# Rotary parts on 128 rows with pages turned in pairs, and GLA level scores written by predicated copies, in a two-layer MLA and GLA step

## The chip, the core and the metric

The kernel runs on one core of a Trainium2 chip. The metric is the device time of one execution in microseconds (us). A core has TensorE (PE, with its weight loads shown apart as PEld), VectorE (DVE), ScalarE (ACT), GpSimd (POOL) and SyncE (SP), each with its own instruction queue, and semaphores between them.

## What is computed

One inference step of two layers. Each layer is FFN half-step, token mixer, FFN half-step, with an RMSNorm before and after each part. Layer 0 mixes by multi-head latent attention (MLA), layer 1 by gated linear attention (GLA). There are 512 prompt tokens and 8 x 8 new tokens of sequences with 2048 cached positions in 16 pages each; model width 1024.

```python
# MLA, prompt: 8 heads, 128 plain and 64 rotary columns
s = (jnp.einsum('bqhd,bkhd->bhqk', qn, k_nope)
     + jnp.einsum('bqhr,bkr->bhqk', qp, k_pe)).astype(jnp.float32) * MLA_SCALE
# MLA, new tokens: latent cache (256) and rotary cache (64), pages by page_table
past_ckv = cache_ckv[page_table].reshape(B, -1, MLA_KV_LORA).astype(c_kv.dtype)
past_kpe = cache_kpe[page_table].reshape(B, -1, MLA_ROPE).astype(k_pe.dtype)
s = (jnp.einsum('bthr,bkr->bhtk', q_lat, all_ckv)
     + jnp.einsum('bthd,bkd->bhtk', q_pe, all_kpe)).astype(jnp.float32) * MLA_SCALE
# GLA: 4 heads, keys of 128, values of 256
diff = G[:, :, None] - G[:, None, :]
decay = jnp.exp(jnp.where(causal[None, :, :, None, None], diff, -jnp.inf))
attn = jnp.sum(qf[:, :, None] * kf[:, None, :] * decay, axis=-1)
```

## The kernel before

**Layout and stages.** Activations are held transposed, features on the 128 partitions and the 576 tokens along the free axis in two halves of 288. Six stages follow each other: FFN, MLA, FFN, FFN, GLA, FFN. Nearly all work is a stream of weight blocks of 128x1024: SP loads a block into `raw` (four slots), ACT writes its high part `w_hi` (L526), POOL its low part `w_lo` (L875), and TensorE forms each product by three matmuls (L1550 to L1552). An output of 288 columns is a *unit*; units go round six PSUM banks, counted by `s_unit` (made by TensorE) and `s_evicted` (emptied by DVE). Every engine's program is written out by hand in stage order; an engine waits on a semaphore, and what is queued behind waits with it.

**MLA, projection.** After the query, key and value blocks, DVE builds the rotary query part `qpe` (64 rows, L1204 to L1208, one sum per head and half, `s_rope`), then copies the new tokens' columns of each head to `q_pes` (L1213, eight copies, `s_qpes`), then empties the key (`kn`, L1218) and value (`vp`, L1223) units. POOL's queue holds only `low(n)` for each block, in order: six down blocks, eight query blocks (uq), two of uk, two of uv.

**MLA, prompt attention.** For 32 steps (8 heads, 4 query blocks of 128, 128 to 512 keys) TensorE forms scores by a product over 128 rows (L1789) and one over the 64 rotary rows (L1790) into one bank, two steps ahead of the transposes of the probabilities (L1815); every fourth step `head_out` follows (L1797). DVE masks (L1245), takes the maximum (L1248), and scales the exponentials (L1258); ACT does the exponential (L708) and copies the transposes (L720).

**MLA, decode.** Batches go in four pairs, each with four groups of four pages. `load_pages` (L361) puts pages into `cache` (four buffers), per group two pages by SP's queue and two by POOL's. For a batch and a group (32 *part-groups*) TensorE transposes the pages: four of 128x128 for each latent half (L1844) and four of 128x64 for the rotary part (L1847), into banks 4, 5 and 6. DVE copies bank 4 (L1268), ACT banks 5 and 6 (L734), to `c_t`. The next part-group's transposes wait for those copies (`s_ctv`, `s_cta`). `group_scores` then forms, for both batches of the pair side by side on 64 columns each, two latent products (L1860) and one over 64 rotary rows (L1862). After four groups come the softmax, the transposes of the probabilities and the products with the pages (L1916). `new_scores` (L1876, L1878) does the same for the eight new tokens.

**GLA.** The chunk scores are made level by level: for each head seven levels (`halves`, L347, splits the tokens into blocks of 2b and compares the second half with the first), and an eighth unit, the diagonal one, which needs no `xl`. A level's operand `xl` (three buffers) takes a difference per half on DVE (`level_dif`, L1358 and L1359), one exponential on ACT (L778), and the products with q on DVE (`q_mul`, L1366) and with k on POOL (`k_mul`, L912). It is begun two levels ahead: at level unit x, DVE issues the difference of x+2, empties unit x, and issues the q product of x+2. TensorE's unit (L1998) waits for both products (L1990 to L1992). DVE empties a unit by a product with the level's 0/1 mask: level 0 into `att_p`, the others into one of two `masked` buffers (L1439), which POOL adds to `att_p` (L933, `g_att`). Levels 4 and up also have a 64-column unit for the new tokens (L2000, L1452; POOL's sum L939, `g_att_s`). The order of the stage is a plan made at build time (L311 to L334): 13 projection blocks (j = 12 to 24) and between them 32 level units, in bursts of two or three:

```python
while j >= 12 and spread and (j + 1 - 12) * (GH * (LEVELS + 1)) > (GH * (LEVELS + 1) - len(spread)) * (GLA_IN - 12):
    kind, hd, lv = spread.pop(0)
    g_plan.append((kind, hd, lv))
```

This gives bursts of 3, 2, 3, 2, 3, 2, 3, 2, 3, 2, 3, 2, 2. POOL takes the `low` of a block (L875) where the plan has that block, between the burst before it and the burst behind it.

## Time and profile before

| | us |
|---|---|
| median of 3 runs (2517.78 to 2524.62) | 2523.54 |
| the profiled execution's own time | 2515.44 |
| its span, first to last instruction | 2513.8 |
| PE busy | 2439.3 (97%) |
| DVE busy | 1019.4 (41%) |
| POOL busy | 852.2 (34%) |
| ACT busy | 789.8 (31%) |

TensorE is busy nearly throughout; matmuls are pipelined, so a busy TensorE isn't one at its peak, and the distance from one start to the next tells more than a duration. The mean granted clock is 0.990 of full speed. FP32 matmuls appear as two records each, transposes as one. Of the chain that ended last 88% is TensorE and 8% DVE.

### The profile page before, as it was taken

What the parts mean: (1) busy time and instruction counts of PE and PEld (TensorE: products, weight loads), DVE (VectorE), ACT (ScalarE), POOL (GpSimd) and SP (SyncE); (2) the same over time, 40 slices, a digit from 0 to 9 for tenths busy, and PEclk for the clock granted to TensorE, in tenths of its full rate; (3) what the DMA queues carried; (4) which work ended last, traced back from release to release, by engine and by line L of the source; (5) the groups of instructions that cost most, each with busy time, mean ns of one, the idle gap of its engine ahead of it and who ended that gap; (6) DMA issues with size and microseconds to landing.
All of it is one profiled execution on the core that took longest, in us unless ns stands there. A gap on an engine that the chain in (4) does not pass through costs nothing.

```text
span 2513.8 us, 43938 instructions
## 1 busy us (share of the span) xinstructions
PE 2439.3 (97%) x17572; PEld 2299.7 (91%) x17572; DVE 1019.4 (41%) x1919; ACT 789.8 (31%) x1392; POOL 852.2 (34%) x477
## 2 busy tenths in 40 slices
PE   8999999899899999999999999999999999999997
PEld 8999999895456999999999999999988799999997
DVE  5332222686332643332254332126577666323223
ACT  5222222414332442222243222224321444222221
POOL 3333333120221133333314333331467423333332
PEclk9999999999999999999999999999999999999999
DMA  3222222130551232222213222222211322222222
GB/s 123 84 84 83 80 84 80 58 115 1 164 172 34 60 91 80 81 83 85 82 58 96 84 80 81 83 86 78 68 51 51 143 85 68 84 83 83 79 86 76
DMA packets 68648, 209.04 MB, mean 83 GB/s; under 512 B 8380, under 2 KB 21181, under 8 KB 68254
## 3 DMA queue, kind: packets, MB, share of 16 engines
q1 hardware_dynamic: 65438, 196.58, 25.5%
q0 software_dynamic: 3072, 10.49, 1.5%
q8 instruction: 103, 1.69, 0.3%
q14 instruction: 35, 0.29, 0.0%
HBM read 199.22 MB, written 7.82 MB: 82 GB/s over the span
## 4 chain that ended last, share of the span: by engine, by line
PE 88%; DVE 8%; ACT 1%; issue 1%; POOL 1%; DMA 0%; POOLq 0%; SPq 0%; DVEq 0%
PE psum L1550 25%; PE psum L1552 25%; PE psum L1551 25%; PE psum L1844 1%; PE psum L1860 1%; DVE h L1016 1%; PE psum L1916 1%; DVE y_ffn L1012 1%; PE psum L1998 1%; DVE x_lo L986 1%; PE psum L1790 1%; DVE work L1007 1%; PE psum L1789 1%; PE psum L1797 1%; DVE w_lo L995 1%
## 5 line engine op out<-in xcount | busy, mean ns | idle before, releaser
L875 POOL TENSOR_TENSOR w_lo<-raw,w_hi 128x1024 fp32r<-128x1024 f32 (+2 forms) x315 | 734.7, 2334 | 1420.0 <-ACT w_hi L526 1420.0
L1550 PE MATMUL psum<-x_hi,w_hi 128*128 128x288 f32 x3568 | 1072.9, 301 | 21.9 <-DVE x_lo L986 17.7
L1552 PE MATMUL psum<-x_hi,w_lo 128*128 128x288 f32 x3568 | 1053.9, 295 | 0.0
L1551 PE MATMUL psum<-x_lo,w_hi 128*128 128x288 f32 x3568 | 1052.9, 295 | 0.0
L1550 PEld LDWEIGHTS psum<-x_hi,w_hi 128*128 128x128 f32 x3568 | 671.7, 188 | 38.5 <-DVE x_lo L986 27.4
L1551 PEld LDWEIGHTS psum<-x_lo,w_hi 128*128 128x128 f32 x3568 | 671.9, 188 | 3.7
L1552 PEld LDWEIGHTS psum<-x_hi,w_lo 128*128 128x128 f32 x3568 | 671.4, 188 | 0.0
L526 ACT ACTIVATE w_hi<-raw 128x1024 fp32r<-128x1024 f32 (+2 forms) x331 | 341.4, 1033 | 797.9 <-DMA raw<-ffn_in 364.2
L1032 DVE TENSOR_TENSOR work<-psum,r_pre 128x288 f32<-128x288 f32 x352 | 160.3, 457 | 659.5 <-PE psum L1552 659.0
L1550 PE MATMUL psum<-gu_hi,w_hi 128*128 128x288 f32 x1408 | 415.5, 295 | 0.0
L1552 PE MATMUL psum<-gu_hi,w_lo 128*128 128x288 f32 x1408 | 414.7, 295 | 0.0
L1551 PE MATMUL psum<-gu_lo,w_hi 128*128 128x288 f32 x1408 | 414.6, 294 | 0.0
L1550 PEld LDWEIGHTS psum<-gu_hi,w_hi 128*128 128x128 f32 x1408 | 264.2, 188 | 0.2
L1551 PEld LDWEIGHTS psum<-gu_lo,w_hi 128*128 128x128 f32 x1408 | 264.1, 188 | 0.2
L1552 PEld LDWEIGHTS psum<-gu_hi,w_lo 128*128 128x128 f32 x1408 | 264.1, 188 | 0.0
L1037 DVE COPY y_ffn<-psum 128x288 f32 (+1 forms) x60 | 27.1, 452 | 366.9 <-PE psum L1552 366.9
L565 ACT ACTIVATE gu_hi<-work 128x288 f32 (+1 forms) x176 | 76.9, 437 | 224.6 <-DVE work L1053 224.6
L1053 DVE TENSOR_TENSOR work<-work 128x288 f32<-128x288 f32 x176 | 116.0, 659 | 28.6 <-ACT work L561 11.5
L561 ACT ACTIVATE work<-work 128x288 f32<-128x288 f32 x176 | 76.3, 436 | 134.0 <-DVE work L1032 133.9
L1048 DVE TENSOR_TENSOR acc<-acc,work 128x288 f32<-128x288 f32 x68 | 89.7, 1319 | 67.2 <-ACT work L570 67.2
L1057 DVE TENSOR_TENSOR gu_lo<-work,gu_hi 128x288 f32 (+1 forms) x176 | 79.3, 453 | 27.8 <-ACT gu_hi L565 26.1
L379 POOL DMA_DIRECT2D cache<-cache x64 | 34.5, 539 | 163.9 <-issue 162.9
(262 smaller groups left out, 1928.4 us busy)
## 6 DMA issues: line engine op xcount, KB each, us to landing
raw<-ffn_in SPq DMA_DIRECT2D x176, 512.0 KB, 3.6
raw<-ffn_out SPq DMA_DIRECT2D x64, 448.0 KB, 3.3
raw<-ffn_out SPq DMA_DIRECT2D x32, 512.0 KB, 3.5
raw<-gla_in SPq DMA_DIRECT2D x25, 512.0 KB, 3.6
cache<-cache SPq DMA_DIRECT2D x64, 160.0 KB, 3.0
cache<-cache POOLq DMA_DIRECT2D x64, 160.0 KB, 3.1
raw<-mla_wo SPq DMA_DIRECT2D x8, 512.0 KB, 3.6
raw<-gla_wo SPq DMA_DIRECT2D x8, 512.0 KB, 3.5
```

The costliest lines, as they stand in the source:

```text
L379: eng.dma_start(cache[b % CACHES][:, 4 * g + i, :], io["cache"][page]).then_inc(landed[bp % (CACHES // 2)][g], 16)
L526: act.activation(w_hi[slot][:, 0:w], raw[slot][:, 0:w], ACT.Copy).then_inc(s_hi, 1)
L561: act.activation(work[:, hf, :], work[:, hf, :], ACT.Silu).then_inc(s_silu, 1)
L565: act.activation(gu_hi[:, i, H[hf]], work[:, 2 + hf, :], ACT.Copy).then_inc(s_guhi, 1)
L875: pool.tensor_tensor(w_lo[slot][:, 0:w], raw[slot][:, 0:w], w_hi[slot][:, 0:w].bitcast(F32), ALU.subtract).then_inc(s_lo, 1)
L1032: dve.tensor_tensor(dst, bank[bk][0:r, 0:HALF], r_pre[0:r, H[hf]], ALU.mult).then_inc(s_evicted, 1)
L1048: dve.tensor_tensor(acc[:, H[hf]], acc[:, H[hf]], work[:, hf, :], ALU.add).then_inc(s_acc, 1)
L1053: dve.tensor_tensor(work[:, 2 + hf, :], work[:, hf, :], work[:, 2 + hf, :], ALU.mult).then_inc(s_gu, 1)
L1057: dve.tensor_tensor(gu_lo[:, pi, H[hf]], work[:, 2 + hf, :], gu_hi[:, pi, H[hf]].bitcast(F32), ALU.subtract).then_inc(s_gulo, 1)
L1550: pe.matmul(out, wh, xh, start=start, stop=False)
L1551: pe.matmul(out, wh, xl, start=False, stop=False)
L1552: return pe.matmul(out, wl, xh, start=False, stop=stop)
```

## The change

Rotary parts: `qpe` and `kpe` get 128 rows, of which POOL sets the lower 64 to zero. Odd pages are read from a second input, `cache_r`, which holds the rotary part ahead of the latent one, so that in `cache` the rotary parts of pages 2i and 2i+1 lie side by side; a transpose of 128x128 turns both. Page 2i's part then stands on rows 0 to 63 and page 2i+1's on rows 64 to 127. `q_pes` has two copies of the query part, one with the upper and one with the lower rows filled, the rest zero, and the rotary scores are two products of 256 columns, whose output goes to every second block of 128 columns. SP loads even pages, POOL odd ones. `c_t` becomes smaller, and `q_pes` lies behind it.

GLA: the difference is taken once over both halves, and ACT's exponential is one instruction per half, with scale -1 on the first. Level 0 is still written by a product with the mask; the other levels are copied straight from PSUM into `att_p` where the mask isn't zero. POOL's sums, the `masked` buffers and the semaphores of both go. SP's loads of the GLA state wait for the first `vt` unit's turn rather than for the sums.

```diff
-        qpe = sb("qpe", [ROPE, HEADS, TOK], offset=g_at + 8 * W4)
+        qpe = sb("qpe", [P, HEADS, TOK], offset=g_at + 8 * W4)
...
-        kpe = sb("kpe", [ROPE, TOK], offset=kv_at + 3 * KT * W4)
+        kpe = sb("kpe", [P, TOK], offset=kv_at + 3 * KT * W4)
...
-        q_pes = sb("q_pes", [ROPE, DEC_BATCH, QR], offset=tail_at)
+        q_pes = sb("q_pes", [P, 2, DEC_BATCH, QR], offset=spare_at)
...
-        c_t = [sb(f"c_t{i}", [P, 3, KEYS], offset=ct_at + i * 12 * KEYS) for i in range(C_TS)]
+        c_t = [sb(f"c_t{i}", [P, 5, KEYS // 2], offset=ct_at + i * 10 * KEYS) for i in range(C_TS)]
...
-            return v[:, :, 0:b], v[:, :, b:2 * b], v[:, :, b - 1:b].to_broadcast([P, n // (2 * b), b])
+            return v[:, :, 0:b], v[:, :, b:2 * b], v, v[:, :, b - 1:b].to_broadcast([P, n // (2 * b), 2 * b])
...
+        def page_part(b, pg, c0, n):
+            c = c0 + ROPE * (pg % 2)
+            return cache[b % CACHES][:, pg, c:c + n]
...
-                        with eng.Fori(lo, hi) as i:
-                            page = eng.value_load(table[0:1, bass.ds(PAGES * b + 4 * g + i, 1)], min_val=0,
+                        with eng.Fori(0, 2) as i:
+                            page = eng.value_load(table[0:1, bass.ds(PAGES * b + 4 * g + odd + 2 * i, 1)], min_val=0,
                                                   max_val=N_POOL - 1)
-                            eng.dma_start(cache[b % CACHES][:, 4 * g + i, :],
-                                          io["cache"][page]).then_inc(landed[bp % (CACHES // 2)][g], 16)
+                            eng.dma_start(cache[b % CACHES][:, 4 * g + odd + 2 * i, :],
+                                          io["cache_r" if odd else "cache"][page]).then_inc(landed[bp % (CACHES // 2)][g], 16)
...
@@ ACT @@
-                        r = P if j == 1 else ROPE
-                        act.activation(c_t[x % C_TS][0:r, j, :], bank[4 + j][0:r, :], ACT.Copy).then_inc(s_cta, 1)
+                        if j == 1:
+                            act.activation(c_t[x % C_TS][:, 2:4, :].rearrange("p a t -> p (a t)"), bank[5],
+                                           ACT.Copy).then_inc(s_cta, 1)
+                        else:
+                            act.activation(c_t[x % C_TS][:, 4, :], bank[6][:, 0:KEYS // 2], ACT.Copy).then_inc(s_cta, 1)
...
-                        act.wait_ge(g_dif, 2 * (i + 1))
-                        act.activation(xl[i % 3][:, 0:n], xl[i % 3][:, 0:n], ACT.Exp).then_inc(g_exp, 1)
+                        act.wait_ge(g_dif, i + 1)
+                        first, second, _, _ = halves(xl[i % 3], lv)
+                        act.activation(first, first, ACT.Exp, scale=-1.0).then_inc(g_exp, 1)
+                        act.activation(second, second, ACT.Exp).then_inc(g_exp, 1)
...
@@ POOL @@
                 for j in range(4, MLA_BLOCKS - DT):
                     low(n0 + j)
-                load_pages(pool, first_unit[st], s_cache_p, SP_PAGES, 4)
+                    if j == MLA_IN + 2:
+                        pool.wait_ge(s_lo, n0 + j + 1)
+                        pool.memset(q_pes[:, :, :, :], 0.0).then_inc(s_zero, 1)
+                        pool.wait_ge(s_zero, 1)
+                        pool.memset(kpe[ROPE:P, :], 0.0).then_inc(s_zero, 1)
+                        pool.wait_ge(s_zero, 2)
+                    if j == MLA_IN + HEADS:
+                        pool.wait_ge(s_lo, n0 + j + 1)
+                        pool.memset(qpe[ROPE:P, :, :], 0.0).then_inc(s_zero, 1)
+                        pool.wait_ge(s_zero, 3)
+                load_pages(pool, first_unit[st], s_cache_p, 1)
...
-                        if c > 0:
-
-                            pool.wait_ge(s_evicted, first_unit[st] + u + 1)
-                            if c > 1:
-                                pool.wait_ge(g_att, n_a)
-                            pool.tensor_tensor(att_p[:, a, :], att_p[:, a, :], masked[:, n_a % 2, :], ALU.add).then_inc(g_att, 1)
-                            n_a += 1
...
@@ DVE @@
                 dve.wait_ge(s_rope, 2 * HEADS)
+                dve.wait_ge(s_zero, 1)
                 for hd in range(HEADS):
-                    dve.tensor_copy(q_pes[:, :, hd * DEC_SEQ:(hd + 1) * DEC_SEQ],
-                                    qpe[:, hd, SEQ:TOK].rearrange("p (b t) -> p b t", t=DEC_SEQ)).then_inc(s_qpes, 1)
+                    for r in range(2):
+                        dve.tensor_copy(q_pes[ROPE * r:ROPE * r + ROPE, r, :, hd * DEC_SEQ:(hd + 1) * DEC_SEQ],
+                                        qpe[0:ROPE, hd, SEQ:TOK].rearrange("p (b t) -> p b t", t=DEC_SEQ)
+                                        ).then_inc(s_qpes, 1)
...
-                        dve.tensor_tensor(x1, ref, g1, ALU.subtract).then_inc(g_dif, 1)
-                        dve.tensor_tensor(x2, g2, ref, ALU.subtract).then_inc(g_dif, 1)
+                        dve.tensor_tensor(x, g, ref, ALU.subtract).then_inc(g_dif, 1)
...
-                            dst = masked[:, n_p % 2, :]
-                            if n_p >= 2:
-
-                                dve.wait_ge(g_att, n_p - 1)
-                        dve.tensor_tensor(dst.rearrange("p (c t) -> p c t", t=P), bk.rearrange("p (c t) -> p c t", t=P), m,
-                                          ALU.mult).then_inc(s_evicted, 1)
+                            dve.wait_ge(s_evicted, u0 + last_lev[a])
+                            dve.copy_predicated(out, m.bitcast(mybir.dt.int32).to_broadcast([P, QB, P]), got
+                                                ).then_inc(s_evicted, 1)
...
@@ PE @@
+                pe.wait_ge(s_zero, 3)
+
...
-                                last = pe.transpose(bank[6][0:ROPE, p * P:(p + 1) * P], cache[b % CACHES][:, pg, KV_LORA:],
-                                                    ident[:, :])
+                            for i in range(2):
+                                last = pe.transpose(bank[6][:, i * P:(i + 1) * P],
+                                                    cache[b % CACHES][:, 4 * g + 2 * i:4 * g + 2 * i + 2, :].rearrange(
+                                                        "p a c -> p (a c)")[:, KV_LORA:KV_LORA + 2 * ROPE], ident[:, :])
...
-                                pe.matmul(out, q_pes[:, b, :], c_t[x % C_TS][0:ROPE, 2, :], start=False,
-                                          stop=True).then_inc(s_score, 1)
+                                r = j - KT
+                                last = pe.matmul(out.rearrange("p (i r t) -> p i r t", r=2, t=P)[:, :, r, :],
+                                                 q_pes[:, r, b, :],
+                                                 c_t[x % C_TS][:, 4, :].rearrange("p (i t) -> p i t", t=P),
+                                                 start=False, stop=r == 1)
```

## Rows read from the trace of the kernel before

**Rows 1.** Busy time by stretch, the GLA level units: length, then each engine, PEclk, DMA, GB/s
```profile
1822.00:1969.00 147.00, 134.77 (x999) 129.71 (x997) 109.38 (x174) 36.67 (x50) 102.86 (x82) 0.95 0.19 58
```

**Rows 2.** Waits of PE, 1822 to 1969 us: us in total, times, longest
```profile
PE psum L1998 <- POOL xl L912: 12.0, 4, 4.2
```

**Rows 3.** Timeline of DVE and of POOL in the level units: start, us, engine, line
```profile
1864.84 2.55 DVE L1358 TENSOR_TENSOR xl<-cum 128x256 f32<-128x256 f32 x1 [0.43 <-PE psum L1998]
...
1864.74 2.37 POOL L875 TENSOR_TENSOR w_lo<-raw,w_hi 128x1024 fp32r<-128x1024 f32 x1
```

**Rows 4.** Busy time by stretch, a stretch of slow clock (columns as in rows 1)
```profile
1918.90:1925.70 6.80, 4.95 (x20) 4.64 (x21) 6.55 (x11) 1.07 (x2) 5.26 (x5) 0.50 0.00 0
```

**Rows 5.** Groups of instructions, 1700 to 2060 us: busy us, mean ns | idle before
```profile
L933 POOL TENSOR_TENSOR att_p<-att_p,masked 128x512 f32<-128x512 f32 x28 | 38.1, 1359 | 1.5 <-DVE masked L1439 1.3
L1358 DVE TENSOR_TENSOR xl<-cum 128x256 f32<-128x256 f32 (+1 forms) x28 | 30.2, 1077 | 5.4 <-PE psum L1998 5.4
L912 POOL TENSOR_TENSOR xl<-xl,qk 128x256 f32<-128x256 f32 (+1 forms) x28 | 29.6, 1056 | 38.5 <-ACT xl L778 38.5
L1359 DVE TENSOR_TENSOR xl<-cum 128x256 f32<-128x256 f32 (+1 forms) x28 | 28.5, 1019 | 0.0
L1439 DVE TENSOR_TENSOR masked<-psum,lmask 128x512 f32<-128x512 f32 x28 | 19.0, 680 | 1.8 <-PE psum L1998 1.8
L778 ACT ACTIVATE xl<-xl 128x512 f32<-128x512 f32 (+1 forms) x28 | 18.3, 654 | 104.9 <-DVE xl L1359 104.9
L1366 DVE TENSOR_TENSOR xl<-xl,qk 128x256 f32<-128x256 f32 (+1 forms) x28 | 12.3, 441 | 4.6 <-ACT xl L778 2.5
L1420 DVE TENSOR_TENSOR kd<-kd,qk 128x576 f32<-128x576 f32 x4 | 2.8, 747 | 0.0
```

**Rows 6.** Timeline of PE and, last, of DVE in the prompt attention (columns as rows 3)
```profile
600.96 0.39 PE L1789 MATMUL psum<-kn,qn 128*128 128x128 f32 x2
601.28 0.48 PE L1790 MATMUL psum<-kpe,qpe 64*128 64x128 f32 x2
601.70 0.55 PE L1815 MATMUL psum<-ident,prob 128*128 128x128 f32 x3
...
603.26 0.66 PE L1815 MATMUL psum<-ident,prob 128*128 128x128 f32 x4
...
634.72 2.32 PE L1797 MATMUL psum<-pt,vp 128*128 128x512 f32 x8
636.88 1.14 PE L1815 MATMUL psum<-ident,prob 128*128 128x128 f32 x7
...
602.72 0.49 DVE L1258 TENSOR_SCALAR prob<-prob,soft 128x512 f32<-128x512 f32 x1
```

**Rows 7.** Timeline of decode, first DVE, then PE (columns as rows 3)
```profile
692.77 0.69 DVE L1268 COPY c_t<-psum 128x512 f32<-128x512 f32 x1
...
693.61 1.06 PE L1844 MATMUL psum<-ident,cache 128*128 128x128 f32 x8
694.51 0.60 PE L1847 MATMUL psum<-ident,cache 128*64 128x128 f32 x4
695.04 1.94 PE L1860 MATMUL psum<-c_t,q_lat 128*64 128x512 f32 x8
696.90 1.07 PE L1862 MATMUL psum<-c_t,q_pes 64*64 64x512 f32 x4
697.91 1.09 PE L1844 MATMUL psum<-ident,cache 128*128 128x128 f32 x8
```

**Rows 8.** Instructions of lines 1213 and 943: duration ns min/median/max, first and last start
```profile
L1213 DVE COPY q_pes<-qpe x8: 177/180/2386, 545.6 to 548.6; 64x64 f32<-64x64 f32 x8
...
L943 POOL MEMSET qg_m<- x1: 1805/1805/1805, 1969.6 to 1969.6; 128x2048 f32 x1
```

**Rows 9.** Groups of instructions by form, 560 to 960 us (columns as rows 5)
```profile
L1933 PE MATMUL psum<-o_lat,uv_f 128*128 128x64 f32 x32 | 3.8, 276 | 1.0 <-DVE o_lat L1323 1.0
...
L1774 PE MATMUL psum<-qn,uk_t 128*128 128x64 f32 x16 | 2.2, 260 | 0.0
```

More of the change, by code:

```diff
@@ L1854, in group_scores @@
                     pe.wait_ge(s_cta, 4 * (step + 1))
-                    for j in range(3):
+                    for j in range(4):
                         for e in range(2):
@@ L1877, in new_scores @@
                             else:
-                                pe.matmul(out, q_pes[:, b, :], kpe[:, SEQ:TOK], start=False, stop=True).then_inc(s_snew, 1)
+                                pe.matmul(out, q_pes[:, 0, b, :], kpe[:, SEQ:TOK], start=False, stop=True).then_inc(s_snew, 1)
                 def fill(bp, f):
```

84 lines of the change are left out of this document (39 added, 45 removed).

## The prediction

> **What bounds the kernel now.** The first view is the table of busy time by stretch. In the 147 us in which the GLA level scores are computed TensorE is busy 134.77 us, DVE 109.38, POOL 102.86, and the mean granted clock is 0.95 [rows 1]. So even here TensorE is the engine that the rest should feed, and there are only two losses to win: its waits and its slow stretches. Off these stages the kernel is a stream of weight blocks that the change doesn't touch.
>
> The view of waits, cut to that stretch, says TensorE waited 12.0 us in 4 waits for POOL's product `xl` (L912), the longest 4.2 [rows 2]. The plan places two or three level units behind each projection block, and `xl` is prepared two levels ahead, beginning when an earlier unit has ended. Only the third unit of a burst of three waits, and two of the six bursts escape because one of their units is the diagonal level, which needs no `xl`: four waits, as counted. They come to 3.0 us on average, which is more than the work of the chain (difference, exponential, product) explains. The timelines of DVE and POOL give the rest: L1358, whose two inputs lie in SBUF, began at 1864.84 beside a POOL subtraction begun at 1864.74, and took 2.55 us, which is until that one ended plus its own work [rows 3]. The group's mean is 1077 ns, that of its twin L1359 1019 [rows 5]. The Trainium skill ("SBUF — State Buffer", "Who interferes with whom") says that a DVE instruction with two SBUF inputs and a GpSimd one that reads SBUF exclude each other for the whole instruction; the rows agree.
>
> The clock: from 1918.9 to 1925.7 it was granted at 0.50, that is 1.2 GHz, right after a wait in a burst [rows 4]. A mean of 0.95 over 147 us is 7.3 us of full-speed work lost [rows 1].
>
> In the prompt attention TensorE alternates a 128-row product (L1789) and a 64-row one (L1790). For 128 columns two records of the first take 0.32 us start to start (600.96 to 601.28), two of the second 0.42 (to 601.70) [rows 6]. With one tile shape there is no such gap: L1797's eight records, two each of 512, 384, 256 and 128 columns, take 2.16 us (634.72 to 636.88) [rows 6], or 0.84 ns a column, so 0.215 us for a pair of 128 columns. The first carries 0.10 too much, the second 0.20.
>
> In decode one group of pages is a chain of transposes (L1844, L1847) and scores (L1860, L1862). L1860's eight records take 1.86 us though the two halves of the columns run side by side (4 x 0.43 = 1.72 by the same rate), and L1862's four take 1.01, not 0.86 [rows 7]: again 0.15 at each change of shape.
>
> **The change, part by part.** Durations are of the profiled execution, 2515.4 us around a span of 2513.8; the median shown is 2523.5, 8.1 more. The differences below are taken from the median.
>
> *Projection (DVE, POOL).* DVE is what ends this stage; TensorE's K units run up to six banks ahead of it. Eight copies q_pes<-qpe become sixteen. Their row has a median of 180 ns and a maximum of 2386 [rows 8], that one being a copy beside a POOL subtraction. A further 8 x 0.18 = 1.4 us is the upper price of unblocked ones; starts overlap, so 0.8 is what I take. POOL gets three zero fills. The nearest is a fill of 128x2048 in 1805 ns, 0.88 ns an element [rows 8]: 0.9 us for q_pes (1024), 0.5 for kpe (576), 4.1 for qpe (4608). The first two stand behind the low part of the third query block, where POOL has time. The third stands ahead of the low part of the second uk block: the three blocks queued behind it (uk, uv, uv) come up to 4 us later and fall on other DVE sums. TensorE has four K units of other weights first, so it doesn't wait. I take +0.7 for the shift, +1.5 in all, and keep -0.5 to +4: the lower end if the copies fall clear of POOL, the upper if one more is blocked for as long as the 2.4 us seen. The same page of the Trainium skill (section as above) says that a copy from SBUF to SBUF excludes any GpSimd instruction, a fill too; the copies come after the fills, so by that rule nothing more is added, but it speaks against putting q_pes's fill later.
>
> *Prompt attention (TensorE).* `qpe` and `kpe` have 128 rows, the lower 64 zero. Columns and count stay, the change of shape goes: 0.10 + 0.20 = 0.30 a step, and I take 0.25. But L1815's transposes need the scaled probabilities: DVE's scaling of 512 ran 602.72 to 603.21 and the transposes began at 603.26 [rows 6], so one step in four is already bound by DVE and wins nothing. 24 x 0.25 = 6.0: -6.0. Ends: 0 (the gap is not the shape) and 32 x 0.30 = -9.6.
>
> *Decode.* Each of the 32 part-groups has two full transposes in place of four 64-column ones (0.53 us, 694.51 to 695.04) [rows 7]. The first of two part-groups wins nothing: its successor waits for DVE's copy, which ended at 693.46 with the successor at 693.61 [rows 7]. The second wins 0.53 - 0.36 = 0.17, where 0.36 is two at 0.11 and one change of shape. So 12 x 0.17 + 3 x 0.2 = 2.6. The gap between L1860 and L1862 goes, 16 x 0.15 = 2.4, less 12 x 0.03 for sharper waiting on DVE. The rotary scores are four pairs of 256 columns in place of two of 512: by the 0.84 ns a column 0.215 us each, so 0.86 + 0.15 against 1.01, no difference. In all -4.6; ends -1 (only the transposes) and -8 (DVE keeps up as well). ACT's copy of that part halves and hides nothing on the path. Page loads keep their sizes and number; even pages go by SP, odd ones by POOL, two each per group as now.
>
> The score's output is now written in two runs of 128 columns with a gap. The nearest rows are 64-column products of one shape: into runs of eight columns with gaps (L1774) 260 ns, into one run (L1933) 276 [rows 9]. So no price. The Trainium skill ("PSUM — Partial Sum Buffer", "Specifications (TRN2)") says instead that any pattern that isn't contiguous slows matmuls significantly; doubling the 64 pairs would be 64 x 0.215 = +14 us, which these rows contradict.
>
> *GLA levels.* POOL loses 28 sums of 1359 ns (38 us) [rows 5] and twelve small ones. DVE's two differences (1077 + 1019) become one of 512 or 576 elements; L1420, 576 elements from SBUF, takes 747 ns [rows 5], so 0.7. ACT's one exponential (654 ns) becomes two of half the length: 0.4 for the first, which is all that POOL's product needs. The predicated copy replaces a product out of PSUM. No row has one; the nearest is the product that it replaces, L1439, also 512 elements out of PSUM, 0.68 us [rows 5], and that is what I take; bounds are 0.5 (only a little below it) and 2 us (three times it): even at 2 us DVE would hold 109.38 - 28 x (2.10 - 0.7) + 28 x 1.3 = 107 us of work in 147. Its added wait is for DVE's own copy of the level before, long done. With POOL free sooner, the weight subtraction runs ahead of the difference instead of over it. The third unit then waits: 0.7 + 0.4 + 1.06 (L912 [rows 5]) + 0.2 for hand-overs = 2.4, less the 0.95 of the unit between (eight records of 128 columns): 1.45 us, four times 5.8. 12.0 becomes 5.8: -6.2. What is late next is the same chain, now bare. Of the 7.3 us of clock I take two thirds back, -5, since the two long waits shrink to a third; ends 0 and -7. GLA together -11.2; ends -3 and -16.
>
> Sum: 1.5 - 6.0 - 4.6 - 11.2 = -20.3, so 2523.5 - 20.3 = **2503.2 us** (2495 against the profiled execution).
>
> **Rivals.**
> *A: the levels stay bound by DVE.* DVE already has 109.38 us of work in 147 [rows 1]; if one difference still falls behind the weight subtraction, waits and slow clock stay. For: the 2.55 us came from that subtraction, not from the removed sums [rows 3]. Against: without the sum (1.36 us [rows 5]) it starts earlier. GLA -3, total -12.1: 2511.4. Chance 0.15.
> *B: the rotary parts win nothing*, because the gaps belong to waits, not to shape. For: one step in four is tight on DVE. Against: L1797 has none [rows 6]. Attention and decode -1 in place of -10.6: total -10.7, 2512.8. Chance 0.12.
> *C: the gap in the score's output costs*, +14 in decode: 2517. Chance 0.04.
> *D: slower, through the predicated copy.* It stands on DVE between the difference and the query product, both of which gate the third unit. It stops being hidden above 1.0 us each: exponential and key product take 0.4 + 1.06, the query product behind it 0.44 (L1366 [rows 5]). At c us it adds 4 x (c - 1.0) in waits, and above 3.4 us DVE is the bound of the stretch: (147 - 107) / 28 = 1.4 over 2. At 5 us it costs 28 x 1.6 + 16 = 61 us, total +40, 2564; the sign turns near c = 3.8. Against: that would be five times L1439's 0.68. Chance 0.04.
> *E: little is seen*, part gains cancelled by a dearer projection (+4) and clock dips elsewhere: 2520. Chance 0.05.
> The forecast itself has 0.60.
>
> **How the numbers follow.** A measurement tells about 0.3%, 7.6 us, from no change: faster means below 2516. The forecast is nearly always below that, A and B four times in five, C and E seldom: 0.60 x 0.96 + 0.27 x 0.8 + 0.01 = 0.80; I say 0.79. Slower: D and a little of E, 0.05. Same: 0.16. The range reaches down to 2490 (attention -8, decode -7, GLA -14 with the clock whole) and up to 2514, which takes in A and B and leaves out C, D, E and the edges.
>
> **What would show it.** POOL's L933 and L939 gone and TensorE's four waits at L1998 near 1.4 us each; no difference on DVE above about 1.5 us; the clock near 0.98 in that stretch. In attention, L1789 and L1790 pairs spaced by 0.21 to 0.25 us at 128 columns, the stage some 6 us shorter, more waits of L1815 for `prob`. In decode, L1860 to the rotary scores in 1.72 us, these in 1.0, and the second part-group's rotary transposes in 0.36. In the projection, DVE reaching the kn copies 1 to 2 us later. The forecast is wrong if the predicated copies take over 1.0 us, if differences still last over 2 us, or if the gap after a change of shape stays with 128 rows.

## The result

The changed kernel takes 2503.86 us, the median of four runs (2497.61 to 2506.89), against 2524.08 us before (four runs, 2517.78 to 2525.13): a ratio of 0.992, 95% interval 0.9905 to 0.9935, or 20.2 us less. A second series gave 0.9914 (0.9900 to 0.9929). The forecast was 2503.2 us.

The profiled pair shows only half of that, 2513.8 against 2503.6 us of span, mostly because the profiled execution of before, at 2515.44 us, was the shortest of that kernel that I have, 8.6 us below its median; that of the changed kernel stood 1.4 us above its own. The stages are therefore read from all profiles together. Each column below is the time from the first TensorE record (product or weight load) of one stage to that of the next, the first column counting from the start of the span: first prompt score (L1789 before, L1795 after), first page transpose, first transpose of the decode output (L1941), first level unit (L2012), first GLA output product (L2037), end. The last column is the time for which the granted clock was 0.50, that is 1.2 GHz ("half clock" below), between decode's end and the first level unit. The kernels of the experiments stand in it too.

| kernel | to prompt scores | prompt attention | decode | to levels | levels | rest | half clock before levels |
|---|---|---|---|---|---|---|---|
| before | 567.0 | 83.6 | 147.1 | 1034.2 | 137.8 | 544.2 | 3.4 |
| after | 572.6 | 78.3 | 141.0 | 1041.3 | 126.2 | 544.3 | 20.5 |
| after_again | 572.6 | 77.8 | 141.0 | 1041.4 | 127.7 | 544.2 | 20.5 |
| rot_only | 572.8 | 77.8 | 140.8 | 1041.3 | 137.8 | 544.2 | 20.5 |
| gla_only | 571.2 | 83.3 | 146.6 | 1034.3 | 126.2 | 544.3 | 3.4 |
| fill_early | 573.9 | 77.8 | 139.9 | 1041.3 | 126.2 | 544.4 | 20.5 |
| copies_late | 567.6 | 78.2 | 139.5 | 1041.3 | 126.2 | 544.3 | 20.5 |
| adds_psum | 570.6 | 78.1 | 143.1 | 1037.8 | 126.1 | 544.2 | 10.2 |
| ahead3 | 572.4 | 77.8 | 141.2 | 1041.3 | 119.7 | 544.4 | 20.5 |
| two_difs | 572.4 | 78.1 | 141.2 | 1034.4 | 129.0 | 544.3 | 3.4 |
| pool_sums | 571.6 | 77.7 | 140.8 | 1041.3 | 131.6 | 544.2 | 20.5 |
| att64 | 572.4 | 83.4 | 141.1 | 1041.3 | 126.2 | 544.3 | 20.5 |
| late_ahead | 568.0 | 78.8 | 139.4 | 1036.4 | 119.7 | 544.2 | 6.8 |
| best | 566.2 | 78.9 | 139.8 | 1037.2 | 119.7 | 544.3 | 10.2 |

Before to after: +5.6, -5.3, -6.1, +7.1, -11.6, +0.1. So 12.7 us of what three stages gain is given back in two others, ahead of the prompt scores and behind decode.

### The profile page after: what moved, and what is told of

Same layout as the page of the kernel before. It is cut to its first block, busy times and chain, and to the rows that moved or that the text cites. A ratio compares the mean times of both kernels' runs of the same rounds, so it can differ in the third digit from the quotient of the medians.

```text
span 2503.6 us, 43881 instructions
## 1 busy us (share of the span) xinstructions
PE 2426.5 (97%) x17572; PEld 2306.8 (92%) x17572; DVE 996.8 (40%) x1899; ACT 786.2 (31%) x1420; POOL 809.6 (32%) x440
## 4 chain that ended last, share of the span: by engine, by line
PE 88%; DVE 9%; issue 1%; ACT 1%; DMA 1%; POOLq 0%; POOL 0%; SPq 0%; DVEq 0%; ACTq 0%
PE psum L1554 26%; PE psum L1556 25%; PE psum L1555 25%; PE psum L1867 1%; PE psum L1930 1%; DVE h L1020 1%; PE psum L2012 1%; DVE y_ffn L1016 1%; DVE x_lo L990 1%; DVE work L1011 1%; PE psum L1849 1%; DVE w_lo L999 1%; PE psum L1803 1%; PE psum L1602 1%; PE psum L1872 1%
## 5 line engine op out<-in xcount | busy, mean ns | idle before, releaser
L882 POOL TENSOR_TENSOR w_lo<-raw,w_hi 128x1024 fp32r<-128x1024 f32 (+2 forms) x315 | 734.6, 2334 | 1425.6 <-ACT w_hi L529 1425.5
L1554 PE MATMUL psum<-x_hi,w_hi 128*128 128x288 f32 x3568 | 1073.8, 301 | 20.2 <-DVE x_lo L990 17.8
L383 POOL DMA_DIRECT2D cache<-cache_r x64 | 34.5, 539 | 161.3 <-issue 161.3
```

Of the source, the lines that this page charges most:

```text
L383: eng.dma_start(cache[b % CACHES][:, 4 * g + odd + 2 * i, :], io["cache_r" if odd else "cache"][page]).then_inc(landed[bp % (CACHES // 2)] ...
L882: pool.tensor_tensor(w_lo[slot][:, 0:w], raw[slot][:, 0:w], w_hi[slot][:, 0:w].bitcast(F32), ALU.subtract).then_inc(s_lo, 1)
L1554: pe.matmul(out, wh, xh, start=start, stop=False)
```

## The profile after

The level units, first the busy time by stretch (columns as in rows 1), then TensorE's waits there (us in total, times, longest), then groups (busy, mean ns | idle before):

```profile
1822.00:1959.00 137.00, 130.80 (x1009) 126.09 (x1007) 85.28 (x146) 39.75 (x78) 56.24 (x43) 1.00 0.22 68
```
```profile
PE psum L2012 <- DVE xl L1372: 5.7, 4, 1.7
```
```profile
L1372 DVE TENSOR_TENSOR xl<-xl,qk 128x256 f32<-128x256 f32 (+1 forms) x28 | 22.9, 819 | 6.4 <-ACT xl L785 5.2
L929 POOL TENSOR_TENSOR xl<-xl,qk 128x256 f32<-128x256 f32 (+1 forms) x28 | 22.5, 802 | 62.2 <-ACT xl L784 62.2
L1442 DVE COPY_PREDICATED att_p<-lmask,psum 128x512 f32<-128x512 int32 x28 | 20.4, 730 | 1.8 <-PE psum L2012 1.8
L1365 DVE TENSOR_TENSOR xl<-cum 128x512 f32<-128x512 f32 (+1 forms) x28 | 19.9, 712 | 5.4 <-PE psum L2012 5.4
L784 ACT ACTIVATE xl<-xl 128x256 f32<-128x256 f32 (+1 forms) x28 | 12.2, 437 | 88.3 <-DVE xl L1365 88.3
```

POOL fell from 102.86 us of work in 147 to 56.24 in 137, the 12.0 us of waits [rows 2] to 5.7, the clock rose from 0.95 [rows 1] to 1.00. Two differences of 1077 and 1019 ns [rows 5] became one of 712, the predicated copy takes 730 ns. The waits' releaser is new: not POOL's key product but DVE's query product, which went from 441 ns [rows 5] to 819. The order of the two products has turned round. Before, DVE's began 0.04 us ahead of POOL's and took 0.42 us, POOL's 0.97. Now POOL's needs only the first exponential and begins 0.26 us ahead, and DVE's, which needs the second, takes 0.75 beside it. Two lines of before, then two of after:

```profile
1834.64 0.42 DVE L1366 TENSOR_TENSOR xl<-xl,qk 128x256 f32<-128x256 f32 x1
1834.68 0.97 POOL L912 TENSOR_TENSOR xl<-xl,qk 128x256 f32<-128x256 f32 x1 [1.36 <-ACT xl L778]
```
```profile
1835.55 0.73 POOL L929 TENSOR_TENSOR xl<-xl,qk 128x256 f32<-128x256 f32 x1 [1.07 <-ACT xl L784]
1835.81 0.75 DVE L1372 TENSOR_TENSOR xl<-xl,qk 128x256 f32<-128x256 f32 x1 [0.19 <-ACT xl L785]
```

Prompt attention and decode, the timeline of TensorE (start, us, engine, line), to be set against [rows 6, 7]:

```profile
595.63 0.39 PE L1795 MATMUL psum<-kn,qn 128*128 128x128 f32 x2
595.85 0.39 PE L1796 MATMUL psum<-kpe,qpe 128*128 128x128 f32 x2
596.08 0.49 PE L1821 MATMUL psum<-ident,prob 128*128 128x128 f32 x3
...
597.74 0.66 PE L1821 MATMUL psum<-ident,prob 128*128 128x128 f32 x4 [0.31 <-DVE prob L1265]
...
691.53 1.09 PE L1849 MATMUL psum<-ident,cache 128*128 128x128 f32 x8
...
693.06 1.07 PE L1849 MATMUL psum<-ident,cache 128*128 128x128 f32 x8 [0.22 <-DVE c_t L1275]
693.96 0.38 PE L1853 MATMUL psum<-ident,cache 128*128 128x128 f32 x2
694.27 1.94 PE L1867 MATMUL psum<-c_t,q_lat 128*64 128x512 f32 x8
696.04 1.03 PE L1872 MATMUL psum<-c_t,q_pes 128*64 128x256 f32 x8
697.00 1.10 PE L1849 MATMUL psum<-ident,cache 128*128 128x128 f32 x8
```

The pair of 128 columns goes 0.22 and 0.23 us, start to start, where it went 0.32 and 0.42. In decode the second rotary transposes take 0.31 (0.53), the latent scores 1.77 (1.86), the rotary scores 0.96 (1.01), and the wait for DVE's `c_t` is now in the record. From one group's first transposes to the next group's it is 5.47 us.

Between the two stages stands the longest wait of TensorE in them, and the change leaves it: the program issues the first page loads only behind the last head's product (at 642.4 us), and TensorE waits 7.65 us for them before and 7.93 after (7.3 to 8.1 in all profiles). It is part of the column of the prompt attention. A second wait for pages follows at the third part-group: 2.3 us after (1.0 to 3.1 with the rotary parts), 0.6 before and in gla_only. So the prediction's "as now" for the page loads holds for sizes and number, not for when the pages are there, and decode's gain is net of that.

```profile
650.60 1.94 PE L1844 MATMUL psum<-ident,cache 128*128 128x128 f32 x8 [7.65 <-DMA cache<-cache]
```
```profile
650.85 1.94 PE L1849 MATMUL psum<-ident,cache 128*128 128x128 f32 x8 [7.93 <-DMA cache<-cache_r]
```

The projection, first POOL's timeline, then DVE's, then what TensorE waited for:

```profile
536.54 3.94 POOL L914 MEMSET qpe<- 64x4608 f32 x1
540.56 2.40 POOL L882 TENSOR_TENSOR w_lo<-raw,w_hi 128x1024 fp32r<-128x1024 f32 x1
...
546.52 2.39 POOL L882 TENSOR_TENSOR w_lo<-raw,w_hi 128x1024 fp32r<-128x1024 f32 x1 [0.97 <-ACT w_hi L529]
```
```profile
537.87 0.45 DVE L1212 TENSOR_TENSOR qpe<-work 64x288 f32<-64x288 f32 x1
...
541.65 1.62 DVE L1212 TENSOR_TENSOR qpe<-work 64x288 f32<-64x288 f32 x1
...
546.93 2.28 DVE L1212 TENSOR_TENSOR qpe<-work 64x288 f32<-64x288 f32 x1
549.25 3.48 DVE L1219 COPY q_pes<-qpe 64x64 f32<-64x64 f32 x16
552.76 4.28 DVE L1225 COPY kn<-psum 128x512 f32<-128x512 f32 x7
```
```profile
PE psum L1554 <- DVE kn L1225: 3.4, 1, 3.4
```

An addition beside the fill (L914) takes 0.45 us; one that meets a weight subtraction (POOL's `w_lo`, L882) stands until that ends. DVE reaches the keys at 552.76, TensorE has waited 3.4 us for the first of them, and then has a stretch at half clock.

Behind decode, busy time by stretch, of before and then of after:

```profile
790.00:795.00 5.00, 5.00 (x50) 3.36 (x48) 0.00 (x0) 2.79 (x3) 4.02 (x2) 1.00 0.00 0
795.00:800.00 5.00, 3.28 (x28) 1.95 (x25) 1.77 (x3) 0.00 (x0) 2.96 (x2) 1.00 0.00 0
800.00:805.00 5.00, 3.59 (x33) 3.45 (x32) 0.69 (x1) 1.44 (x2) 0.00 (x0) 1.00 0.00 0
```
```profile
785.00:790.00 5.00, 5.00 (x50) 3.26 (x48) 0.00 (x0) 1.69 (x2) 5.00 (x3) 1.00 0.00 0
790.00:795.00 5.00, 3.28 (x24) 2.23 (x20) 1.77 (x3) 0.00 (x0) 1.85 (x1) 0.90 0.01 2
795.00:800.00 5.00, 5.00 (x25) 5.00 (x25) 0.00 (x0) 0.00 (x0) 0.00 (x0) 0.50 0.00 0
800.00:805.00 5.00, 3.59 (x16) 3.40 (x16) 0.69 (x1) 1.54 (x2) 2.37 (x1) 0.50 0.01 3
```

The same work, 3.28 us busy out of 5 at decode's last waits, is followed by full clock before and by 0.50 after. This stretch is 13.7 us long and so costs at most half of that; a second one, near 1763 us, is 6.8 us long where before has 3.4. Together they are the +7.1 us.

## The experiments

**The changed kernel again (after_again).** No edit.

> The changed kernel once more, on the same chip and in the same rounds as the three beside it. Expected 2504 us, 0.990 to 0.994 of before. If the half-clock stretches fall at the same places of every execution of this kernel, its profile again has one in the projection (before the first attention score) and one behind the last pair of decode, some 31 us lost to the clock in all (25 in the kernel before); if they are a matter of chance, their places and their sum differ from those of the first profile, and the medians of single runs scatter by the granted clock alone.

2503.29 us, ratio 0.9914 (0.9900 to 0.9929). Every stage came out within 0.5 us of the first profile, save the levels (127.7 us), which have one half-clock stretch. The dips ahead of the prompt scores and behind decode are at the same places. Executions differ with the clock: at a mean granted clock of 0.991 this kernel took 2497.6 and 2499.3 us, at 0.987 and 0.988 between 2503.8 and 2506.9.

**One half of the change at a time (rot_only, gla_only).** Of the diff, all that touches `qpe`, `kpe`, `q_pes`, `c_t` and the pages in the one; the joined difference, the exponentials, the predicated copies and the removed sums in the other.

> The change's rotary parts alone (128-row attention scores, pairs of pages turned at once, both kinds of page), level scores as before on POOL. By the stages of the two profiles the rotary parts give +5.6 (projection), -5.6 (prompt attention), -6.1 (decode), so 6.1 us less than before at an equal clock, and the stretch behind decode at half clock takes it back: 2518 to 2524 us, 0.998 to 1.000 of before. The rival, by the prediction's own terms (+1.5, -6.0, -4.6): 9 us less, 2515 us, if the +5.6 of the projection belongs to something that the GLA part brings (it has no instruction there, so I give that little). In its profile the first attention score comes at 572.5 us and GLA's third level units wait for POOL as before, 12 us over four.

> The change's GLA part alone (one joined difference, two exponentials, predicated copies, no sums on POOL), rotary parts as before. By the stages 11.5 us less: 2512 us, 0.995 to 0.996 of before; first attention score at 567.0 us. If most of GLA's gain is its two half-clock stretches, which might come back when the stages ahead of it end at another time, only the 6.2 us of waits stay: 2517 us. In the profile: wait of the third level unit of each head 5.7 us over four, behind the q product on DVE.

rot_only: 2512.8 us, 0.9954 (0.9938 to 0.9970). gla_only: 2509.06 us, 0.9948 (0.9934 to 0.9962). The table adds up by stage: 77.8 and 140.8 us belong to the rotary parts, 126.2 to GLA's. GLA's gain doesn't depend on when the stages ahead end. The medians don't add up: the two halves win 10.6 and 14.4 us, 25.0 together, where both at once win 20.1; stage times from one profile each can't say where the 5 us went. Three expectations were off. rot_only's gain in the medians, 10.6 us, is larger than its profile's, whose execution was with two others at a clock of 0.986 and 2516 to 2517 us, against 2507.5 to 2509.3 at 0.990 and 0.991. gla_only, forecast at 2512 us, is 3 us faster than that in the median. And it has its first prompt score at 571.2 us instead of 567.0, although it changes nothing there. 2.4 us of it arose ahead of the first rotary addition (507.36 us, 504.97 before), 1.7 of them at the kernel's first weights. The additions then took 4.0 us more, this group in place of 11.7 us and 729 ns before, and the eight copies behind them 2.2 less, as none of them met a subtraction:

```profile
L1193 DVE TENSOR_TENSOR qpe<-work 64x288 f32<-64x288 f32 x16 | 15.7, 980 | 2.1 <-DVE work L1190 0.5
```

So which additions meet a weight subtraction differs from execution to execution, and a difference of a few us in this stage, from one pair of profiles, isn't all the change's.

**The fill earlier (fill_early).**

```diff
-                    if j == MLA_IN + HEADS:
+                    if j == MLA_IN + 3:
                         pool.wait_ge(s_lo, n0 + j + 1)
                         pool.memset(qpe[ROPE:P, :, :], 0.0).then_inc(s_zero, 1)
```

> The changed kernel with the zero fill of rows 64 to 127 of the prompt's rotary queries moved from behind the low half of block 4+HEADS to just behind the two other fills, where POOL has nothing to do. Theory: the 3.94 us fill held back three low halves, and DVE's copies beside them stretched, so that the no-rotary keys came 4 us late and PE waited 3.4 us: the first attention score comes back from 572.6 to 568 to 569 us, and the kernel takes 3.5 to 5 us less than the change (ratio to the changed kernel 0.998, 2499 to 2501 us). Rival: the lateness comes from the sixteen copies of the decode queries (3.5 us for 16 against 3.1 for 8) and from the first unit at half clock: then the first attention score stays at 571 to 572.6 us, no gain above 1 us.

2505.4 us, 0.9922 (0.9905 to 0.9938), first prompt score at 573.9 us. My theory fell: moving the late fill wins nothing, and the rival, the sixteen copies, was left. The subtractions no longer wait for the fill, but the additions meet them all the same:

```profile
537.18 2.39 POOL L882 TENSOR_TENSOR w_lo<-raw,w_hi 128x1024 fp32r<-128x1024 f32 x1 [1.02 <-ACT w_hi L529]
```
```profile
537.55 2.33 DVE L1212 TENSOR_TENSOR qpe<-work 64x288 f32<-64x288 f32 x1
...
550.68 3.48 DVE L1219 COPY q_pes<-qpe 64x64 f32<-64x64 f32 x16
554.19 4.47 DVE L1225 COPY kn<-psum 128x512 f32<-128x512 f32 x7
```

**The copies later (copies_late).**

```diff
-                for hd in range(HEADS):
-                    for r in range(2):
-                        dve.tensor_copy(q_pes[...], qpe[...]).then_inc(s_qpes, 1)
...
                         dve.tensor_copy(vp[:, t, b * 512:(b + 1) * 512], bank[u % RING]).then_inc(s_evicted, 1)
+                        hd = QB * b + t
+                        for r in range(2):
+                            dve.tensor_copy(q_pes[...], qpe[...]).then_inc(s_qpes, 1)
```

> The changed kernel with the sixteen copies of the decode queries taken out of the row ahead of the no-rotary keys' evictions and put, two each, behind the eight evictions of the values; the zero fill stays where the change has it. Theory: the projection's extra time is DVE's lateness at those keys (its additions held beside POOL's low halves, then 3.5 us of copies), TensorE waits 3.4 us for the first of them and then has a stretch at half clock that costs 1.7 us more. With the copies out of the way that wait goes: first attention score at 567.5 to 569 us instead of 572.6, the kernel 3.5 to 5 us below the changed one where its other half-clock stretches stay as they are. Rival: the copies only move, and TensorE waits for the values instead (each then takes 0.69 + 0.43 us of DVE where its unit comes every 1.8 us): start at 571 us or later.

2500.79 us, 0.9908 (0.9894 to 0.9922); first prompt score at 567.6 us, 5.0 earlier, and no wait for a key or a value. DVE now has time behind each key:

```profile
547.07 3.08 DVE L1220 COPY kn<-psum 128x512 f32<-128x512 f32 x5
550.51 0.69 DVE L1220 COPY kn<-psum 128x512 f32<-128x512 f32 x1 [0.35 <-PE psum L1556]
...
554.59 0.69 DVE L1225 COPY vp<-psum 128x512 f32<-128x512 f32 x1 [0.67 <-PE psum L1556]
```

The profile answers the theory: the copies between the last addition and the keys are what makes TensorE wait. The additions took as long as in after_again (12.1 and 12.2 us), and the keys began at 547.07 us instead of 552.82. The two later kernels with this edit agree (568.0 and 566.2 us; the nine with the rotary parts and without it stand at 570.6 to 573.9). The median can't tell this kernel from the changed one, the intervals overlap.

**One operand out of PSUM (adds_psum).**

```diff
-                        ta, tb = work[0:ROPE, 2 * hf, :], work[0:ROPE, 2 * hf + 1, :]
+                        ta, tb = ps[0:ROPE, 0:HALF], work[0:ROPE, hf, :]
...
-                        dve.tensor_tensor(qpe[0:ROPE, hd, H[hf]], ta, tb, ALU.add).then_inc(s_rope, 1)
+                        dve.tensor_tensor(qpe[0:ROPE, hd, H[hf]], ta, tb, ALU.add).then_inc(s_evicted, 1)
```

> The changed kernel with the first product of each rotary query written back into its PSUM bank, so that the addition behind it reads one operand out of PSUM and one out of SBUF instead of two out of SBUF; the work is the same, the bank is given back by the addition. Theory: an addition with both operands in SBUF does not run beside a POOL operation of that kind but stands until it ends (0.45 us alone, 0.8 to 2.6 us beside a low half in the changed kernel). Then all sixteen additions take 0.4 to 0.6 us, the copies start 3 to 5 us earlier and the first attention score comes at 567 to 569 us. Rival: they are held by something else they share with POOL (any access to SBUF, or memory traffic): then additions of 1.5 us and more stay, and the start at 571 to 574 us.

2501.61 us, 0.9905 (0.9890 to 0.9921). The groups:

```profile
L1218 DVE COPY q_pes<-qpe 64x64 f32<-64x64 f32 x16 | 7.3, 454 | 0.5
L1211 DVE TENSOR_TENSOR qpe<-psum,work 64x288 f32<-64x288 f32 x16 | 7.2, 449 | 0.6
```

All sixteen additions take 0.45 us, 7.2 us together against 14.4 in the changed kernel's profile, although those at 541.21 and 542.56 stood beside a subtraction. The copies, which now came earlier, met the subtractions in their place (two took 2.3 us each), so the keys began at 550.8 us and the first prompt score at 570.6, between the two expectations. Both kinds of instruction are held by POOL, and each shows it alone. The Trainium skill ("SBUF — State Buffer", "Who interferes with whom") says the same: a DVE instruction with two SBUF inputs contends with a GpSimd one that reads SBUF but not with one that only writes, and a copy can use two ports and contend as well. The 0.45 us beside the fill, above, and the 0.45 us with a PSUM operand, here, agree with it.

**Level operands three ahead (ahead3).** DVE, ACT and POOL alike:

```diff
-                            for i in range(2):
+                            for i in range(3):
                                 level_dif(i)
                                 q_mul(i)
...
-                            level_dif(xi + 2)
+                            level_dif(xi + 3)
```

> The changed kernel with GLA's level operands prepared three ahead instead of two, in the three buffers that are there. Theory: of the four waits that are left (5.7 us, at the third level unit) the cause is order and not speed: DVE takes the difference of the third level only when it has waited for the first unit. With three ahead these waits go, 5 to 5.7 us less in GLA (first level unit to first output product 126.2 -> 120.5 to 121.5 us), the kernel 4 to 5.7 us below the changed one. Rival: DVE is too slow for the levels (difference 0.7, product or copy 0.7, query product 0.8 a level, against some 2 us of TensorE in the dense part): the same wait then comes at the fourth unit, with 1 us gained or nothing.

2498.14 us, 0.9888 (0.9871 to 0.9906), an interval that still touches the changed kernel's; the levels take 119.7 us, 6.5 less (more than the 5 to 5.7 expected), and TensorE has no wait for `xl` in them. late_ahead and best show the same 119.7. In the changed kernel DVE waited for the first unit with a buffer free and began the third difference at 1834.33. Here it is done by then, and even a difference that is held for 2.50 us beside a subtraction is hidden:

```profile
1831.40 0.68 DVE L1365 TENSOR_TENSOR xl<-cum 128x512 f32<-128x512 f32 x1
1832.87 0.76 DVE L1372 TENSOR_TENSOR xl<-xl,qk 128x256 f32<-128x256 f32 x1 [0.79 <-ACT xl L785]
1833.55 0.81 DVE L1036 TENSOR_TENSOR vt_f<-psum,r_pre 128x288 f32<-128x288 f32 x2
1834.28 2.50 DVE L1365 TENSOR_TENSOR xl<-cum 128x512 f32<-128x512 f32 x1
```

So the waits that the change had left were a matter of order, and nothing on DVE is too slow for them.

**Which half of the GLA part (two_difs, pool_sums).** The first keeps the predicated copies and puts back two differences and one exponential; the second keeps the joined difference and puts back the masked buffers and POOL's sums.

> The changed kernel with the predicated copies kept and the two half differences and the one exponential of before put back. It tells the two halves of the GLA part apart. If the sums on POOL were the whole cause of the 12.0 us of waits, the waits stay near 5.7 to 6.5 us and the stage from first level unit to first output product takes 126 to 127.5 us. If the joined difference is half of it (two differences held beside POOL took 1077 and 1019 ns each against 712 ns for one), the waits are 8 to 10 us and the stage takes 129 to 130 us.

> The changed kernel with the joined difference and the two exponentials kept, but the level scores masked into two buffers by DVE and summed on POOL again, small ones too: the counterpart of the run with two differences. There the sums' absence alone gave 127.3 us of the stage's 130.9 to 126.2 at equal clock, with waits of 7.1 us. Theory: the sums on POOL are the larger part, so with them back the stage is at 129 to 131 us net of half-clock stretches and the third level units wait 9 to 12 us, behind POOL's product. Rival: with the joined difference the two parts overlap, either alone would have given most: then the stage stays below 128 us and the waits below 8.

two_difs: 2506.83 us, 0.9928 (0.9915 to 0.9941). pool_sums: 2507.63 us, 0.9932 (0.9915 to 0.9948). TensorE's waits, the first row of two_difs, the second of pool_sums:

```profile
PE psum L2012 <- POOL xl L928: 7.1, 4, 2.0
```
```profile
PE psum L2031 <- DVE xl L1389: 8.1, 4, 2.7
```

From 12.0 us the removed sums alone lead to 7.1 and the joined difference alone to 8.1, both to 5.7. The gains of the halves, 4.9 and 3.9, don't add to 6.3: they overlap. The stage took 129.0 and 131.6 us, with 3.4 and 6.8 us of half clock in it, where before had 137.8 with 13.7 and after 126.2 with none. Of the sizes I had expected, 6.5 or less or 8 and more for two_difs, 9 to 12 or below 8 for pool_sums, each wait lies between the two theories: neither half alone is the cause, and the sums are the larger one by 1 us, from one profile of each.

**Prompt scores on 64 rows (att64).**

```diff
-                    pe.matmul(out, qpe[:, hd, i * P:n], kpe[:, 0:n], start=False, stop=True).then_inc(s_s, 1)
+                    pe.matmul(out, qpe[0:ROPE, hd, i * P:n], kpe[0:ROPE, 0:n], start=False, stop=True).then_inc(s_s, 1)
```

> The changed kernel with the prompt's rotary score products back on 64 rows (operands cut to rows 0 to 63), all else as changed; the fills stay. Theory: the price of before is the change of rows from product to product in one score, 32 pairs with two changes each, and nothing else in the stage: first attention score to first page transpose goes from 77.8 to 78.3 us back to 83.3 to 83.8 us (at equal clock loss), and the wait of the transposes for DVE's probabilities (3.3 us, 8 times in the changed kernel) falls back below 1 us; the kernel is 5 to 6 us slower than the changed one. Rival: part of the 5.6 us came from elsewhere in the stage (the earlier end of the fills, other phases of DVE): then less than 4 us comes back.

2511.02 us, 0.9944 (0.9927 to 0.9961), 7 us above the changed kernel where 5 to 6 were expected. The stage takes 83.4 us again, the others are unchanged, and TensorE's wait for DVE's probabilities, 3.3 us in 8 in the changed kernel, is back at once:

```profile
PE psum L1821 <- DVE prob L1265: 0.7, 1, 0.7
```

The rows are therefore the whole of that stage's gain, 5.1 to 5.6 us.

**Two edits together, and four (late_ahead, best).** late_ahead has the edits of copies_late and ahead3; best has those of adds_psum and fill_early as well.

> The changed kernel with two edits: the decode queries' copies behind the values' evictions, and the level operands three ahead. Their gains lie in stages apart from each other and should add: first attention score at 567.5 us (-5.1), first level unit to first output product 119.7 us (-6.5): 11.6 us less than the changed kernel at an equal clock, 2490 to 2493 us, 0.986 to 0.988 of before. Rival: an earlier end of a stage only moves half-clock stretches into the next, as behind decode: then 3 to 5 us of it go and the median is 2495 to 2497 us.

> The same two edits, and the rotary additions reading one operand out of PSUM, and the zero fill earlier. With the copies out of the way DVE is no longer late at the keys, so the two further edits should win nothing that TensorE waits for: within 1.5 us of the kernel with two edits, all sixteen additions at 0.45 us. Rival: the wait for the query evictions that is left there (1.0 us, once) goes as well and the first attention score comes at 566.5 us.

late_ahead: 2490.65 us, 0.9868 (0.9848 to 0.9888). best: 2487.0 us, 0.986 (0.9842 to 0.9878). The first adds up: 568.0 and 119.7 us in its two stages, 13 us below the changed kernel's medians, 11.6 expected. The last two edits take the first prompt score to 566.2 us, since the one wait left for a query eviction (0.9 us) goes too, so there the rival was right; the medians, 3.7 us apart, don't tell the two kernels apart, as their intervals overlap. Both beat the changed kernel, as their intervals show.

## Why the prediction was right, and where it was not

The forecast of 2503.2 us lies 0.7 us from the median, and that closeness is luck: the terms measured in the profiled pair come to -10.2 us, not -20.3, because the projection cost 4.1 us more than its term and a stage without a term cost 7.1. The other 10 us of the medians come from where the two profiled executions stand among their kernels' runs. What made before's so short isn't known, since no other profile of before exists. Both things that rival E named, a dearer projection and dips of the clock elsewhere, came true in the profiled pair, though not in the medians, where E expected 2520. And the range's lower end of 2490 was not what its own gains give: -8, -7 and -14 from 2523.5 make 2494.5.

*GLA levels* (-11.2 forecast, -11.6 in the profiles). The waits were to fall to 5.8 us and fell to 5.7, the clock was to give 5 us and gave about as much (-11.6 less 6.3). The chance of rival A went by: with the sums gone one of 28 differences touched a subtraction, for 0.15 us, and none took over 0.76. The copy took 0.73 us, against 0.68 taken from L1439 and 2 as upper bound, far below the point where rival D begins. One step was wrong without harm: I let POOL's key product (1.06 us) end the chain. It ended at DVE's query product, which begins 0.26 us later and goes slower beside it: key product 0.80 us and query product 0.82 on average. The two mistakes cancel, so the 0.1 us between forecast and measured wait is luck too.

*Prompt attention* (-6.0; -5.3 and -5.8). The gaps at changes of rows were what they seemed, as att64 shows, and the steps bound by DVE exist: 8 waits in 32, my one in four. Rival B fell here.

*Decode* (-4.6; -6.1). The term was sized too small. A group went from 5.83 us (692.08 to 697.91, of which [rows 7] has the second part) to 5.47: 0.22 for the transposes (0.31 us against my 0.36), 0.09 for the latent and 0.05 for the rotary scores. That is 0.36 a group, 5.8 for sixteen, where mine was 0.29 a group; that the first part-group wins nothing was right (1.53 us both times). The gap in the output costs nothing, so rival C fell: eight records took 0.96 us. The Trainium skill ("PSUM — Partial Sum Buffer", "Specifications (TRN2)") expects a pattern that isn't contiguous to slow matmuls significantly; in runs of 128 columns the measurement decides against it. Decode alone wasn't undone in an experiment; that its gain is there in rot_only and att64 (140.8 and 141.1 us) and not in gla_only (146.6) ties it to the page pairs. The later pages, above, are inside the -6.1.

*Projection* (+1.5, at most +4; +5.6). This is the step that failed. I added "+0.7 for the shift" and 0.8 for eight copies, as if DVE's lateness passed one to one to TensorE. The runs show instead: DVE was 4.0 us later at the keys (548.78 to 552.76); TensorE, up to then ahead, ran out of banks and waited 3.4 us; then it had 3.4 us at half clock, at most 1.7 us more. Of the 4.0 us, 0.8 stood already at the first addition (504.97 to 505.77). The rest is the copies' price together with one meeting: POOL's last subtraction (546.09 us before, 546.52 after) holds whichever DVE instruction it meets for some 2.3 us. In before that was one of the eight copies (3.11 us in all), in after the last addition, so the additions look 2.8 us dearer and the copies only 0.37; in after_again it was a copy again, and there sixteen copies took 5.59 us and the additions 12.2, near before's 11.7. With no copy held it is 3.48 us for sixteen (after) and 0.90 for eight (gla_only). So the term that was mis-sized is that of the copies: 0.8 forecast, 2.5 to 2.6 measured. After_again's and gla_only's lines:

```profile
547.20 5.59 DVE L1219 COPY q_pes<-qpe 64x64 f32<-64x64 f32 x16
```
```profile
552.12 0.90 DVE L1198 COPY q_pes<-qpe 64x64 f32<-64x64 f32 x8
```

The fill, which I made the source of the shift, doesn't give the time back when it is moved (fill_early). The copies do (copies_late), since they stand between the additions and what TensorE waits for. Chance stays in the held additions: they took 11.7 us in before, 15.7 in gla_only without any edit near them, and 12.2 and 14.4 in two executions of the changed kernel. But the first prompt score came at 572.6 us in both of those.

*Between decode and the levels* (no term; +7.1). No part of my sum looked at a stage that the change doesn't touch. In 8 of the 12 profiles with the rotary parts, and in neither without, this stage took 1041 us with 20.5 us at half clock; in the four others it took 1034 to 1038. Why the chip fell to 1.2 GHz there stays open: the busy time ahead of it looks alike. Seven of the eight profiles stand above their kernels' best runs and may owe it to this stretch, but copies_late's is its kernel's fastest and has it; how often it falls in executions without a profile no run shows.

The profiled pair has 48.8 and 61.0 us of half clock in its spans. With half of that taken off, an upper bound for its cost, it goes from 2489.4 to 2473.1 us, -16.3; my terms without the clock are 1.5 - 6.0 - 4.6 - 6.2 = -15.3. That is the fairer test of the sum, and there the sum is off by 1 us, with the projection's cost and decode's gain both put too low.

## What to carry to other kernels

A wait for an operand that is prepared ahead asks first for the order of the queue: one more level prepared in buffers that lay there took away 5.7 us of waits, more than either half of the rewriting did alone (4.9 and 3.9). Work that nobody waits for soon, such as the decode copies, belongs behind the evictions that TensorE needs, or a small lateness becomes a wait and often a slow clock too (of nine profiles with a wait of 2 us or more for the keys, eight had a half-clock stretch behind it, att64 none). And an instruction on DVE with two SBUF operands should be priced beside what POOL reads at that time, or be given one operand in PSUM.

## What was not expected

- The additions' price depended on the execution, not on the program: 11.7, 12.2, 14.4 and 15.7 us for the same sixteen instructions in four profiles. What one of them escaped, a copy behind it could meet.
- A product written back into its own PSUM bank cost as much as one into SBUF (0.45 us), and freed the addition behind it from POOL entirely.
- The half-clock stretch behind decode returned with the same length, 13.7 us, some 2 us behind decode's end, in the eight profiles named above, wherever that end lay (785.3 to 796.9 us), and was absent in two_difs, whose decode ended at 791.7 us, as the changed kernel's did (791.8).
